# Seven-product FFN: weight sums one per step and a pair ahead, activations scaled on ScalarE first, a fourth activation part made ahead

## The reference

```python
def swiglu(x, w_gate, w_up, w_down):
    return (jax.nn.silu(x @ w_gate) * (x @ w_up)) @ w_down

for layer in range(DEPTH):                       # DEPTH = 2
    hdn = rmsnorm(x, gains[0])
    x = x + 0.5 * rmsnorm(swiglu(hdn, w_gate[layer, 0], w_up[layer, 0], w_down[layer, 0]), gains[1])
    hdn = rmsnorm(x, gains[2])
    mix = mixer_ab(hdn, ...) if layer % 2 == 0 else mixer_c(hdn, ...)
    x = x + rmsnorm(mix, gains[3])
    hdn = rmsnorm(x, gains[4])
    x = x + 0.5 * rmsnorm(swiglu(hdn, w_gate[layer, 1], w_up[layer, 1], w_down[layer, 1]), gains[5])
```

## Time and profile before

| | us |
|---|---|
| median of 3 runs | 2627.71 (2626.11 to 2627.72) |
| the profiled execution | 2626.2 |
| its span | 2624.6 |
| TensorE busy | 2493.1 |
| VectorE busy | 1655.9 |
| ScalarE busy | 1065.3 |
| GpSimd busy | 410.7 |
| mean granted clock of TensorE | 0.989 of full speed |

### The profile page before, as it was taken

How to read it: one execution, slowest core, us unless ns; L and a number is a source line. 1 busy time by engine, 2 the same in 40 slices (tenths; PEclk the granted TensorE clock), 3 DMA queues, 4 the chain that set the end, 5 groups by cost and what they waited for, 6 DMA issues and landing times. The chain is left out here.

```text
span 2624.6 us, 50609 instructions
## 1 busy us (share of the span) xinstructions
PE 2493.1 (95%) x19669; PEld 2346.4 (89%) x19669; DVE 1655.9 (63%) x2874; ACT 1065.3 (41%) x2026; POOL 410.7 (16%) x601
## 2 busy tenths in 40 slices
PE   8999999998999989999998999999989989999998
PEld 7899999995557989999998999999979969899998
DVE  6888525546664688862588872467546666888723
ACT  4444324114443444442444442334354444444422
POOL 0000003023331200000200000255245532000001
PEclk9999999999999999999999999999999999999999
DMA  4233422248994123342123343223210133233431
GB/s 115 81 97 97 113 81 73 76 131 295 305 304 153 58 73 97 97 116 86 50 72 97 97 112 87 65 71 84 66 35 1 34 105 97 74 87 97 111 88 46
DMA packets 397837, 264.15 MB, mean 101 GB/s; under 512 B 10984, under 2 KB 370613, under 8 KB 397608
## 3 DMA queue, kind: packets, MB, share of 16 engines
q1 hardware_dynamic: 386096, 223.03, 30.1%
q0 software_dynamic: 11536, 38.28, 4.4%
HBM read 251.71 MB, written 9.56 MB: 100 GB/s over the span
## 5 line engine op out<-in xcount | busy, mean ns | idle before, releaser
L763 PE MATMUL ps<-x_part_hi,part_hi 128*128 128x272 f32 x2016 | 593.5, 294 | 43.0 <-DVE scratch L981 22.8
L763 PE MATMUL ps<-x_part_hi,part_lo 128*128 128x272 f32 x2016 | 584.2, 290 | 0.0
L763 PE MATMUL ps<-x_part_lo,part_hi 128*128 128x272 f32 x2016 | 581.9, 289 | 0.0
L507 DVE TENSOR_TENSOR w_lo<-w_raw,w_hi 128x1024 fp32r<-128x1024 f32 (+1 forms) x170 | 245.8, 1446 | 490.0 <-ACT w_hi L500 487.8
L500 ACT CAST w_hi<-w_raw 128x1024 fp32r<-128x1024 f32 (+1 forms) x170 | 199.0, 1170 | 641.8 <-PE ps L535 582.6
L763 PEld LDWEIGHTS ps<-x_part_hi,part_hi 128*128 128x128 f32 x2016 | 380.5, 189 | 59.8 <-DVE scratch L981 33.3
L763 PEld LDWEIGHTS ps<-x_part_lo,part_hi 128*128 128x128 f32 x2016 | 381.3, 189 | 0.0
L763 PEld LDWEIGHTS ps<-x_part_hi,part_lo 128*128 128x128 f32 x2016 | 380.4, 189 | 0.0
L1479 POOL TENSOR_TENSOR xT<-xT,rstd_rows 128x272 f32<-128x272 f32 x96 | 84.5, 910 | 1687.3 <-DVE rstd_rows L1504 1687.3
L535 PE MATMUL ps<-hd_hi,w_hi 128*128 128x272 f32 x1408 | 294.2, 290 | 4.4 <-DVE w_lo L507 4.3
L535 PE MATMUL ps<-hd_lo,w_hi 128*128 128x272 f32 x1408 | 291.6, 289 | 0.0
(11 more groups left out here) (575 smaller groups left out, 4473.3 us busy)
## 6 DMA issues: line engine op xcount, KB each, us to landing
w_raw<-in_ffn_w_down_dram SPq DMA_DIRECT2D x64, 704.0 KB, 4.5
w_pair<-in_ffn_w_gate_dram SPq DMA_DIRECT2D x72, 512.0 KB, 4.1
w_pair<-in_ffn_w_up_dram SPq DMA_DIRECT2D x72, 512.0 KB, 5.1
v_pages<-in_cache_a_v_dram POOLq DMA_DIRECT2D x128, 256.0 KB, 4.4
w_raw<-in_c_w_in_dram SPq DMA_DIRECT2D x33, 512.0 KB, 4.0
k_pages<-in_cache_a_k_dram SPq DMA_DIRECT2D x64, 256.0 KB, 4.3
k_pages_raw<-in_cache_a_k_dram SPq DMA_DIRECT2D x64, 256.0 KB, 4.2
w_raw<-in_ab_w_in_dram SPq DMA_DIRECT2D x25, 512.0 KB, 3.9
```

The costliest lines, as they stand in the source:

```text
L507: e.tensor_tensor(w_lo[:, n % 2, 0:nk * P], raw[:, n % RAW, 0:nk * P], w_hi[:, n % 2, 0:nk * P].bitcast(F32), ALU.subtract).then_inc(sem(" ...
L763: mm = e.matmul(ps[:, bank, 0:TH], w[:, k * P:(k + 1) * P], x[:, k, :], start=idx < 4 and k == 0 and w is wh and x is xp_hi[idx], stop=k = ...
```

## The change

- The weight sums t4, t3, t2, t1 stand in four steps one after another (after products 5, 6, 0 and 1 of a pair), and t3, t2 and t1 are made for the pair after the one they were made for at that place (`sum_due`).
- Scaling by the gain goes to ScalarE (`xg`: 16 activations in four groups), VectorE multiplies each group of four tiles by the row factors in one instruction of 1088 columns (`xn`).
- `EARLY` = 4: four x_parts lie in `h_lo`, which moves LATE from 10 to 6. So there are 16 late tiles instead of 12, and pair_high and pair_low remain for one pair instead of three.
- `low` 0 to 3 go to pair 3; gate 3, up 3 and hidden 3 come one step later; x_part 6's low half comes one step later and its high half before the loop; parts 0 to 3 of pair 0 are made in a row after t3 and t2, with t1 behind part 0.

The core of the diff:

```diff
-LATE = 10
+LATE = 6
+EARLY = 4
-        x_at = [at_hl + LATE * T * 4 + 2 * x * QUARTER for x in range(3)] + [at_hd + 2 * x * QUARTER for x in range(4)]
+        x_at = [at_hl + LATE * T * 4 + 2 * x * QUARTER for x in range(EARLY)]
+        x_at += [at_hd + 2 * x * QUARTER for x in range(PROD - EARLY)]
+        def sum_due(q, what):
+            if q < RING:
+                pair = {"t4": 0, "t3": 1, "t2": 1, "t1": 1}[what]
+                return pair if q == ("t4", "t3", "t2", "t1").index(what) else None
+            p, idx = (q + RING) // PROD, (q + RING) % PROD
+            pair = p if what == "t4" else p + 1
+            return pair if idx == 3 + ("t4", "t3", "t2", "t1").index(what) and pair < WP else None
-            return {1: (0, 1), 2: (2, 3), 3: (4,), 4: (5, 6), 5: (7, 8)}.get(q - PROD * WP + RING + 1, ())
+            return {0: (0, 1), 1: (2, 3), 2: (4, 5), 3: (6,), 4: (7, 8), 5: (9, 10)}.get(q - PROD * WP + RING + 1, ())
+        X_NORMED = ((2, 1, 0, 0), (0, 0, 0, 0), (6, 1, KH, 1), (4, 0, KH, 0))
 @@ act_x_part @@
-            if x >= 3:
+            if x >= EARLY:
                 e.wait_ge(sem("unit_done"), g["first"] + 4 * STD)
 @@ act_gate_up @@
+            def xg(n):
+                part, h, k0, negative = X_NORMED[n]
+                for k in range(k0, k0 + KH):
+                    of = neg_gains[:, KH * f + k - KH:KH * f + k - KH + 1] if negative else gain(l, n_pre, k)
+                    ins = e.activation(x_sums[:, part, k - k0, :], xT[:, k, half(h)], ACT.Copy, scale=of)
+                ins.then_inc(sem("ffn_scalar"), did("scalar", "xg", n))
+            if s:
+                xg(0)
             act_split(e, first + 2, 0, KD)
...
             act_split(e, first + 3, 0, KD)
+            if s == 0:
+                e.wait_ge(sem("mean_ready"), 1)
+                xg(0)
+            xg(1)
+            xg(2)
+            xg(3)
             silu(0)
...
-            act_x_part(e, g, 1)
-            act_x_part(e, g, 2)
+            for n in (1, 2, 3):
+                act_x_part(e, g, n)
...
-            for q in range(3):
+            for q in range(4):
                 act_part(e, g, q)
-            for n in (3, 4):
-                act_x_part(e, g, n)
-                act_part(e, g, n)
+            act_x_part(e, g, 4)
+            act_part(e, g, 4)
             act_x_part(e, g, 5)
+            act_x_part(e, g, 6)
 @@ dve_gate_up @@
-            def xn(part, h, k0, n, of):
-                for k in range(KH):
-                    e.scalar_tensor_tensor(x_sums[:, part, k, :], xT[:, k0 + k, half(h)], of(k0 + k), rb[:, half(h)],
-                                           ALU.mult, ALU.mult).then_inc(sem("ffn_vector"), did("vector", "xn", n + k))
+            def xn(n):
+                part, h, _, _ = X_NORMED[n]
+                wait_step(e, "scalar", f, "xg", n)
+                e.tensor_tensor(x_sums[:, part, :, :], x_sums[:, part, :, :], rb[:, half(h)].unsqueeze(1).to_broadcast([P, KH, TH]),
+                                ALU.mult).then_inc(sem("ffn_vector"), did("vector", "xn", n))
...
+            dve_x_part(e, g, 3)
             hidden(2)
-            low(0)
-            low(1)
-            dve_part(e, g, 0)
             dve_t3(e, g, 0)
             dve_t2(e, g, 0)
-            dve_part(e, g, 1)
+            dve_part(e, g, 0)
             dve_t1(e, g, 0)
-            dve_part(e, g, 2)
-            dve_x_part(e, g, 3)
-            dve_part(e, g, 3)
-            dve_t4(e, g, 0)
+            for q in (1, 2, 3):
+                dve_part(e, g, q)
             dve_x_part(e, g, 4)
             dve_part(e, g, 4)
             dve_x_part(e, g, 5)
             for q in range(PROD * WP):
...
+                if q == 2:
+                    dve_x_part(e, g, 6)
                 if q + RING < PROD * WP:
                     dve_part(e, g, q + RING)
-                    if (q + RING) % PROD == 0:
-                        dve_t3(e, g, (q + RING) // PROD)
-                        dve_t2(e, g, (q + RING) // PROD)
-                    if (q + RING) % PROD == 1:
-                        dve_t1(e, g, (q + RING) // PROD)
-                    if (q + RING) % PROD == 3:
-                        dve_t4(e, g, (q + RING) // PROD)
-                if q == 1:
-                    dve_x_part(e, g, 6)
-                if q == 3:
+                if sum_due(q, "t4") is not None:
+                    dve_t4(e, g, sum_due(q, "t4"))
+                if sum_due(q, "t3") is not None:
+                    dve_t3(e, g, sum_due(q, "t3"))
...
+                if q == 4:
                     gate(3)
                     up(3)
-                if q == 5:
+                if q == 6:
                     hidden(3)
-                if q in (2 * PROD, 2 * PROD + 1):
-                    low(2 + q - 2 * PROD)
+                if p == 3 and idx in (1, 2):
+                    low(idx - 1)
+                if p == 3 and idx in (4, 5):
+                    low(idx - 2)
```

More of the change, by code:

```diff
@@ L628, in vector_steps @@
+                steps += [(x, sum_due(q, x)) for x in ("t4", "t3", "t2", "t1") if sum_due(q, x) is not None]
+                steps += {4: [("gate", 3), ("up", 3)], 6: [("hidden", 3)]}.get(q, [])
+                steps += [("low", {1: 0, 2: 1, 4: 2, 5: 3}.get(idx))] * (p == 3 and idx in (1, 2, 4, 5))
                 steps += [("late", x) for x in late_at(q) if q < PROD * WP - 1]
-            return steps + [("gated", KU - 1)] + [("late", x) for x in range(7, KF - LATE)]
+            return steps + [("gated", KU - 1)] + [("late", x) for x in range(9, KF - LATE)]
@@ L947, in act_gate_up @@
             act_split(e, first + 4 * STD + 1, 0, KU)
-            for x in range(9, KF - LATE):
+            for x in range(11, KF - LATE):
                 act_late(e, f, x)
```

57 lines of the change are left out of this document (26 added, 31 removed).

## The result

The changed kernel takes **2601.93 us** (median of 4 runs, 2599.96 to 2603.47) against 2627.72 before (2626.11 to 2627.74): ratio 0.9903, 95% interval 0.9886 to 0.992. That is 25.8 us less, where 26.9 were worked out.

What follows compares the result with a forecast made beforehand. With TensorE busy 95%, only its standstills or lower-clock time could be won, mostly waits for VectorE's sums. 6.8 us per stage, four times 27.2, less 1.5, plus 1.2, gave 26.9 us: 2601 us, range 2590 to 2617.

Steps and rivals of the forecast that it cites:

- Step 1: Product stages: weight sums one per step bring pairs 8 on to 10.67 us, about 1.6 us won per stage.
- Step 2: Product stages: LATE 10 to 6 takes pair_high and pair_low from pairs 4 and 6; pair 6 wins 2.3 us.
- bound for a missing cover: End of the product stage: four more late copies and subtractions cost nothing, without cover up to 4 times 0.63 us.
- Step 3: Low 0 to 3 moved to pair 3: pair 2 wins 2.8 us, pair 3 loses 0.3, pair 4 wins 0.9.
- Step 4: Start of the stage: pair 0 comes to 16.0 to 16.5 us, 0.7 lost; bounds 2.5 lost and 3 won.
- rival C: Half the gain, by longer queues at pairs 3 to 5 or a lower clock: 2608 to 2620 us, chance 0.19.
- Step 5: Scaling on ScalarE: unit 4 of the first sublayer 1.5 us late, hidden in sublayers 2 to 4 with 2.6 us to spare.
- Step 6: Last sublayer's down start: part 125 is made earlier, so the down weights load earlier; 1.2 us won.
- Step 7: Product stages: t3, moved ahead of its pair's first part, has its weight load covered by 0.9 us.
- rival E: Slower: a pair's load lands after VectorE reaches t3, holding up parts, u_sum and w_sum; 2633 us and more, chance 0.05.

Runs made afterwards that it cites:

- e3: The changed kernel with the weight sums back at their old places in VectorE's order: 2619.9 us, ratio 0.9956 to the kernel before.
- e11: The kernel before with only LATE set to 6 and x_part 3 made early on ScalarE: 2609.5 us, ratio 0.9935.
- e2: The changed kernel with LATE 10 and EARLY 3 put back: 2606.8 us, ratio 0.9917 to the kernel before.
- e4: The changed kernel with the scaling of the activations back on VectorE: 2602.2 us, ratio 0.9900 to the kernel before.

## Why the prediction was right, and where its steps were not

The total is right within 1.1 us of 26.9 by the medians, and that is in part luck. For the profiled run, for which the sum was made, the gain is 23.0: 22.7 in the product stages, where 27.2 were worked out. There the two largest errors, 4 and 5.8 us, stand against each other. The main mechanism was right: VectorE's weight sums stood ahead of quarter and w_sum, and spreading them took TensorE's waits away. Point by point, with the mean of the four stages:

- **Step 1, sums one per step, 1.6 us a stage in pairs 8 on.** The pairs came to 10.59, not 10.67, which makes 2.6 us. The step that failed is "0.09 to 0.10 is the step from the seventh product to the next pair, which I leave in place". It isn't a step between pairs: it is the price of a product that had to wait, and it went with the wait. In the changed kernel pair 4's product 5 shows it (TensorE's timeline, the wait in brackets):

```profile
135.63 0.39 PE L773 MATMUL ps<-x_part_hi,part_hi 128*128 128x272 f32 x1 [1.40 <-DVE rstd_rows L998]
135.86 0.29 PE L773 MATMUL ps<-x_part_lo,part_hi 128*128 128x272 f32 x1
135.98 0.28 PE L773 MATMUL ps<-x_part_hi,part_lo 128*128 128x272 f32 x1
```

  The first two matmuls are 0.23 us apart and the next 0.12; that product takes 1.60 to 1.61 in place of 1.51. In the kernel before product 6 of every pair waited, so that the extra stood always between product 6 and the next pair.
- **Step 2, LATE, pair 6 from 13.04 to 10.7.** Pair 6 is at 10.59. Pair 7, which the sum left out, fell by 0.17. But the cause was booked to one part where two remove it: spread sums alone bring it to 11.03, LATE alone to 10.94. The late tiles cost nothing, as said: the last six products of a stage take 9.08 us as before. But that holds only with the spread sums. With 16 late tiles and the sums at their old places they take 9.8 to 10.1 us (e3, e11), 0.7 us a stage that the prediction's bound for a missing cover had in view. The x_part that is early with it is worth 1.0 us in pair 0, by e2.
- **Step 3, low parts: pair 2 2.8 won, pair 3 0.3 lost, pair 4 0.9 won.** Measured 2.6 won, 0.6 lost, 0.8 won. The times of the pairs were right because the whole new queue had been written out. The name on them was wrong: of pair 2's gain the spread sums give 1.6 by themselves and the moved low parts 0.6, and at pairs 3 and 4 the low parts cost 1.3 to 1.8 us.
- **Step 4, start of the stage, pair 0 at 16.0 to 16.5, 0.7 lost.** It came to 16.17 to 16.70, 0.8 lost, the starts of products 5, 6 and 7 being 3.0 to 3.6, 2.76 and 4.34 us behind the one before, where the working makes 2.8, 2.8 and 4.2 (its losses on top of 1.51). What it missed lies one pair on: pair 1 was booked 0.1 faster and is 1.4 us slower, by the lower clock behind the wait for up 3. The price of a slow stretch stood in rival C, with the earlier trace rows as its row; the stretch in that row cost nothing itself, as pair 0 of the kernel before shows, but in pair 1 four of them cost 6.1 us, near C's 6.4. It was not carried into the sum, though step 4 had found the wait that sets it off. The 5.8 us by which pair 1 misses its booking are the largest single error, and step 1's extra 4 us hid most of it.
- **Step 5, scaling.** Unit 4 of the first sublayer is waited for 1.40 us (1.5 worked out), and product 0 starts 1.8 us later. In the other sublayers it is hidden. In the second ScalarE makes the last scalings by 905.93, splits unit 4 from 906.38 on, and VectorE's half ends at 908.67 (907.44 plus 1.23). Unit 4 starts at 911.29, 2.6 us later, the margin that was worked out:

```profile
904.18 1.75 ACT L898 ACTIVATE x_sums<-xT,gains 128x272 f32<-128x272 f32 x4
...
906.38 1.03 ACT L502 CAST w_hi<-w_raw 128x1024 fp32r<-128x1024 f32 x1
...
907.44 1.23 DVE L509 TENSOR_TENSOR w_lo<-w_raw,w_hi 128x1024 fp32r<-128x1024 f32 x1 [1.49 <-ACT w_hi L502]
...
911.29 0.42 PE L537 MATMUL ps<-hd_hi,w_hi 128*128 128x272 f32 x2
```

  What the double product's 497 ns on VectorE became is 508 ns on ScalarE plus a quarter of 1284 on VectorE: more engine time in all, and worth nothing even to VectorE's queue (e4). "Perfetto Trace Analysis" of the Trainium skill (Optimizing Scalar/DVE Operations) says that offloading to ScalarE may make sense if VectorE is saturated. The trace agrees with the condition: ahead of product 0 VectorE is busy 43.5 of 50.2 us even with the scaling on it (e4, second sublayer), TensorE doesn't wait for it there, and moving the work brings nothing.
- **Step 6, last sublayer's down start, 1.2 won.** ScalarE's wait for the down weights is 2.16 us after 3.07: 0.9 won.

```profile
2444.11 1.37 ACT L502 CAST w_hi<-w_raw 128x1408 fp32r<-128x1408 f32 x1 [2.16 <-DMA w_raw<-in_ffn_w_down_dram]
```

- **Step 7, loads.** Over 72 executions t3 waits 2.4 us in all for its load, three times: 1.0 and 1.1 us for pair 0, ahead of the stage, and once in the loop, 0.22 us at 236.34, which reached no product. So the loads were covered, and rival E didn't come.

```profile
L827 DVE TENSOR_TENSOR w_sums<-w_pair 128x512 f32<-128x512 f32 x72 | 49.4, 686 | 2.4 <-DMA w_pair<-in_ffn_w_gate_dram 2.1 <-DMA w_pair<-in_ffn_w_up_dram 0.2
```

Two sums of the prediction are off without bearing on the result: 126 times 1.51 is 190.3 and not 190.6, and in rival E, at 56 us for each us past 7.4, the whole gain is gone at 7.9 and not at 8.

So the result is right as a sum over pairs, but for pair 1, and wrong as a sum over parts. Per pair the working was within 0.3 us except in pair 1. Per part, the three alone give 24.6, 16.6 and -5.3 us, 35.9 together, where the change gives 25.8: two of them empty the same queue, and the third and the new order at the start give some back.
